# Row spread of the SSD mixer in four row groups and four banks, weight slots on 512-byte multiples, and another order of steps

## What is computed

```python
for l in range(DEPTH):                                   # DEPTH = 2
    h = rms_norm(x, attn_norm_w[l])
    proj = h @ w_in[l]                                   # 1024 x 2444
    a_q, a_k, a_v, b_z, b_xbc, b_dt, c_q, c_k, c_v = jnp.split(proj, offsets, axis=-1)
    y_a = windowed_gqa_sink(...)                         # 6 heads of 64
    y_b = ssd_mixer(b_z, b_xbc, b_dt, ...)               # 6 heads of 64, forward and backward
    y_c = diff_attention(...)                            # 4 heads of two maps of 32
    x = x + jnp.concatenate([y_a, y_b, y_c], axis=-1) @ w_out[l]
    h = rms_norm(x, ffn_norm_w[l])
    x = x + hierarchical_moe(h, ...)                     # 32 experts, 6 MB of weights each

# in ssd_mixer, for each of 6 heads and 2 directions:
da = jnp.cumsum(dt * a)                                  # over the tokens
seg = da[:, :, :, None, :] - da[:, :, None, :, :]        # every pair of tokens
decay = jnp.exp(jnp.where(lower, seg, -jnp.inf))
y_diag = jnp.einsum('bclsh,bcshp->bclhp', (C B^T) * decay, x * dt)
```

## Time and profile before

| what | value |
|---|---|
| median of three runs | 1198.58 us (1197.28 to 1199.71) |
| the profiled execution's own time | 1195.88 us, of which its span 1194.2 us |
| TensorE matmul busy | 933.3 us, 78% of the span |
| VectorE / ScalarE busy | 353.7 us (30%) / 203.0 us (17%) |
| bytes moved | 436.17 MB, mean 365 GB/s |
| mixer stage of layer 0 / of layer 1 | about 11 to 158 us / 600 to 747 us |

### The profile page before, as it was taken

The page is one execution under the profiler, slowest core; times in us unless marked ns, Lnnn a source line. Parts: engine busy times, 40 slices in busy tenths (PEclk is TensorE's granted clock), DMA queues, the critical chain, the costliest instruction groups (busy, mean ns, idle before and its releaser), DMA issues.

```text
span 1194.2 us, 26453 instructions
## 1 busy us (share of the span) xinstructions
PE 933.3 (78%) x11004; PEld 593.6 (50%) x11004; DVE 353.7 (30%) x1161; ACT 203.0 (17%) x600; POOL 8.0 (1%) x24
## 2 busy tenths in 40 slices
PE   7999989667668786796799998986667666665854
PEld 6887755334334443453388777443334333333532
DVE  4656352111112222132155654321111111111213
ACT  2366211000001010010024652110000000000001
POOL 2000000000000000000000000000000000000000
PEclk9998989888789998998899999898787888888988
DMA  9853389999999999999997235899999999999995
GB/s 328 313 234 142 109 337 426 426 426 426 426 425 423 426 426 425 401 423 428 409 374 312 82 131 232 349 424 426 427 426 426 427 426 426 428 423 427 425 425 215
DMA packets 50633, 436.17 MB, mean 365 GB/s; under 512 B 9408, under 2 KB 13760, under 8 KB 24640
## 3 DMA queue, kind: packets, MB, share of 16 engines
q1 hardware_dynamic: 50496, 434.26, 87.8%
HBM read 433.20 MB, written 1.05 MB: 364 GB/s over the span
## 4 chain that ended last, share of the span: by engine, by line
PE 48%; DMA 36%; issue 5%; DVE 5%; SPq 3%; DVEq 2%; ACT 1%; another core or an unknown queue 0%; ACTq 0%
DMA ring<-in_w_up 32%; PE ps L622 14%; PE ps L710 7%; PE ps L638 5%; PE ps L853 5%; DMA ring<-in_w_down 3%; PE ps L647 3%; PE ps L590 3%; PE ps L726 2%; SPq L461 1%; PE ps L610 1%; PE ps L715 1%; SPq L463 1%; DMA ring<-in_w_in 1%; PE ps L822 1%
## 5 line engine op out<-in xcount | busy, mean ns | idle before, releaser
L622 PE MATMUL ps<-ring,xg 128*32 128x256 f32 x4352 | 319.8, 457 | 174.5 <-DMA ring<-in_w_up 166.6
L622 PEld LDWEIGHTS ps<-ring,xg 128*32 128x32 f32 x4352 | 173.0, 131 | 304.5 <-issue 245.2
L1203 DVE SCALAR_TENSOR_TENSOR th<-th,ps 128x128 f32<-128x128 f32 x72 | 20.7, 288 | 592.3 <-ACT th L975 592.3
L638 PE MATMUL ps<-ring,actT 128*32 128x256 f32 x2304 | 139.5, 382 | 14.2 <-issue 12.9
L975 ACT ACTIVATE th<-ps 128x128 f32<-128x128 f32 x72 | 20.0, 278 | 514.9 <-PE ps L622 480.1
L638 PEld LDWEIGHTS ps<-ring,actT 128*32 128x32 f32 x2304 | 68.9, 109 | 75.6 <-DVE actT L1207 22.6
L590 PE MATMUL ps<-xh,Pb 128*32 128x256 f32 x1152 | 80.7, 397 | 24.5 <-issue 21.3
L710 PE MATMUL ps<-hT,ring 128*128 128x256 f32 x416 | 93.3, 381 | 1.3 <-ACT hT L1012 0.8
L710 PEld LDWEIGHTS ps<-hT,ring 128*128 128x128 f32 x416 | 78.0, 190 | 14.6 <-issue 4.0
L647 PE MATMUL ps<-ysb,PwT 32*128 32x256 f32 x992 | 71.5, 402 | 0.0
L590 PEld LDWEIGHTS ps<-xh,Pb 128*32 128x32 f32 x1152 | 39.4, 113 | 49.1 <-issue 26.0
(11 more groups left out here) (259 smaller groups left out, 690.0 us busy)
## 6 DMA issues: line engine op xcount, KB each, us to landing
ring<-in_w_down SPq DMA_DIRECT2D x62, 2048.0 KB, 41.0
ring<-in_w_gate SPq DMA_DIRECT2D x60, 2048.0 KB, 45.0
ring<-in_w_up SPq DMA_DIRECT2D x60, 2048.0 KB, 46.5
ring<-in_w_in SPq DMA_DIRECT2D x6, 2048.0 KB, 16.5
ring<-in_w_out SPq DMA_DIRECT2D x4, 2048.0 KB, 19.6
ring<-in_w_gate SPq DMA_DIRECT2D x8, 1024.0 KB, 30.0
ring<-in_w_up SPq DMA_DIRECT2D x8, 1024.0 KB, 31.7
ring<-in_w_in SPq DMA_DIRECT2D x6, 1024.0 KB, 16.4
```

Of the source, the lines that this page charges most:

```text
L622: last = mm(b_gate[j * SLOTS:(j + 1) * SLOTS, 0:2 * GQ], tokens[:, k, :], ring[:, low:high + 1:high - low, o:o + GQ], start=(k == 0), stop ...
L638: last = mm(b_y[j * SLOTS:(j + 1) * SLOTS, 0:DQ], actT[:, c * SLOTS:(c + 1) * SLOTS], ring[:, slot, o:o + DQ], start=(c == 0), stop=(c == ...
```

## The change

- `ROWS` becomes `3 * 32 + 2 * S_H` = 108. The last loop of `dta` writes the 12 values four times instead of twice, at columns 0, 32, 64 and 96, so that `cumT` holds its sums on four groups of partitions.
- `rows.k` takes each of its four rows (two heads, two directions) from a group of its own and writes each to a bank of its own, columns 0 to 255. `tenants` gives it four banks. `seg.h.d` reads bank `("seg", h, d)`.
- The start of `ring` is rounded up to a multiple of 512 bytes. Before, it was a multiple of 64; by the sizes of what lies below it, it began 192 bytes past a multiple of 512.
- `ORDER` is another permutation of the same steps. Up to `par` and from `outA.3` on it is the same.

```diff
-ROWS = 32 + 2 * S_H
+ROWS = 3 * 32 + 2 * S_H
...
 ORDER = """
-    sq xT.0 xT.1 xT.2 xT.3 rs par xbc.3 xbc.0 conv.3 xbc.2 xbc.1 conv.0 silu.0 xbc.4 conv.2 conv.1 dc.0 conv.4 silu.1
-    aq.0 silu.2 silu.3 dc.1 dt silu.4 dta aq.2 ak cB cum cumT xs.0 aS.0 sc.0 sc.1 cb.0 seg.0.0 nm.0 nm.1 seg.0.1 seg.1.0
-    rows.0 row.0.0 z.0 row.0.1 aq.1 zs.0 pT.0 xs.1 v seg.1.1 sc.2 row.1.1 aS.1 row.1.0 sc.3 ck.0 y.0 cb.1 rows.1 seg.2.0
-    seg.2.1 z.2 lam yq.0 pT.1 seg.3.0 row.2.0 nm.2 row.2.1 seg.3.1 row.3.1 row.3.0 z.1 zs.2 zs.1 sc.4 seg.4.0 seg.5.0
-    nm.3 pT.2 row.4.0 seg.4.1 yq.1 aS.2 seg.5.1 rows.2 ck.1 sc.5 y.1 row.5.0 row.4.1 row.5.1 oa.0 cq.1 cq.0 nm.4 y.2
-    pT.3 yq.2 nm.5 cS.0 oa.1 sc.6 pT.4 pT.5 sc.7 sS nm.6 oa.2 yn sc.8 cS.1 sc.9 pT.6 sc.10 nm.7 sc.11 outA.0 pT.7 sc.12
-    nm.8 outA.1 od.0 pT.8 sc.13 outA.2 nm.9 pT.9 od.1 oS.0 oS.1 outA.3 cn outB.0 outB.1 outB.2 outB.3 xc2.0 xc2.1 xc2.2
-    sa.0 sa.1 xc2.3 sa.2 fT.0 sd fT.1 fT.2 fT.3 rs2 lg seed wt cnt xn2 rank ov route
+    sq xT.0 xT.1 xT.2 xT.3 rs par xbc.0 xbc.3 conv.0 xbc.2 silu.0 conv.3 xbc.1 aq.0 dc.1 conv.2 conv.1 lam xbc.4 silu.1
+    silu.2 conv.4 dc.0 dt silu.3 dta silu.4 ak aq.2 cum cB sc.0 aS.0 sc.1 cumT nm.0 cb.0 z.0 zs.0 seg.0.0 seg.0.1
+    row.0.1 v rows.0 aq.1 row.0.0 seg.1.0 seg.1.1 xs.0 pT.0 row.1.0 xs.1 row.1.1 sc.2 sc.3 seg.2.0 nm.1 aS.1 ck.0 nm.2
+    y.0 cb.1 rows.1 row.2.0 nm.3 yq.0 z.2 seg.3.0 seg.2.1 row.2.1 aS.2 seg.3.1 row.3.0 row.3.1 pT.1 sc.4 seg.4.0 zs.2
+    nm.4 z.1 seg.4.1 seg.5.0 zs.1 rows.2 y.1 seg.5.1 yq.1 ck.1 row.4.0 row.4.1 row.5.1 cq.0 row.5.0 pT.2 oa.0 sc.5 cq.1
+    y.2 pT.3 cS.0 nm.5 yq.2 pT.4 oa.1 sc.6 sc.7 sS cS.1 pT.5 nm.6 yn oa.2 pT.6 sc.8 sc.9 nm.7 sc.10 outA.0 pT.7 outA.1
+    sc.11 nm.8 sc.12 pT.8 sc.13 nm.9 od.0 outA.2 pT.9 oS.0 od.1 oS.1 outA.3 cn outB.0 outB.1 outB.2 outB.3 xc2.0 xc2.1
+    xc2.2 sa.0 sa.1 xc2.3 sa.2 fT.0 sd fT.1 fT.2 fT.3 rs2 lg seed wt cnt xn2 rank ov route
 """
...
     if step[0] == "rows":
-        return [("seg", 2 * step[1] + 1, d) for d in range(2)]
+        return [("seg", 2 * step[1] + a, d) for a in range(2) for d in range(2)]
...
+        base[0] = -(-base[0] // 512) * 512
         ring = sb("ring", [P, RING + LATE, CHUNK])
...
                         for a in range(2):
                             for d in range(2):
-                                r = slice(32 * d, 32 * d + 2 * S_H)
-                                c = 32 * d + d * S_H + 2 * s[1] + a
-                                last = mm(ps[BANK["seg", 2 * s[1] + 1, d]][:, a * SEQ:(a + 1) * SEQ],
+                                o = 32 * (2 * a + d)
+                                r = slice(o, o + 2 * S_H)
+                                c = o + d * S_H + 2 * s[1] + a
+                                last = mm(ps[BANK["seg", 2 * s[1] + a, d]][:, 0:SEQ],
                                           ident[r, c:c + 1].broadcast_to([2 * S_H, P]), cumT[r, d, :], start=True, stop=True)
...
-                        e, seg_rows, c = E[h % 2][d], ps[BANK["seg", h | 1, d]], d * S_H + h
-                        for t in range(TT):
-                            o = h % 2 * SEQ + t * P
-                            A(e[:, 2 * t, :], seg_rows[:, o:o + P], ACT.Relu, bias=cum[:, t, 0, c:c + 1], scale=-1.0)
-                        o = h % 2 * SEQ + (1 - d) * P
+                        e, seg_rows, c = E[h % 2][d], ps[BANK["seg", h, d]], d * S_H + h
+                        for t in range(TT):
+                            A(e[:, 2 * t, :], seg_rows[:, t * P:(t + 1) * P], ACT.Relu, bias=cum[:, t, 0, c:c + 1], scale=-1.0)
+                        o = (1 - d) * P
                         A(e[:, 1, :], seg_rows[:, o:o + P], ACT.Exp, bias=cum[:, d, 2, c:c + 1])
...
-                        for o in (0, ROWS - n):
+                        for o in range(0, ROWS, 32):
                             last = v.tensor_tensor(dta[:, :, o:o + n], dts[:, :, :],
                                                    aneg[:, :].unsqueeze(1).broadcast_to([P, TT, n]), ALU.mult)
```

## The result

The changed kernel takes 1185.64 us (median of four runs, 1185.0 to 1186.87) against 1199.14 us of the kernel before (1197.28 to 1200.2 over four runs). The ratio is 0.9894, 95% interval 0.9877 to 0.991: 13 us less, about two and a half times the 5.2 us that were forecast. The profiled execution took 1185.0 us with a span of 1183.3; before it was 1195.88 and 1194.2, so the two traces differ by 10.9 us, while the medians differ by 13.5. The trace of before is of a short execution of its kernel (1195.88 us, under the lowest of the four runs), the one after of an ordinary one; the 2 to 3 us between are in neither trace.

A forecast was written before the change was run, and what follows sets the result against it. Mixer stages bound by TensorE, expert stages by DMA. Spread 2.7, gap before `y.2` 0.4, tail 1.6, others 0, plus 0.5 for the clock: 5.2 us off, 1193.4 against the median; forecast 1191 to 1196, 8 in 10 from 1184 to 1199.

The forecast's parts named there:

- The bound: Whole kernel: time cut from a mixer stage comes off the total one for one; expert stages take what their bytes take.
- The spread: `rows.k` in four row groups: half the streaming, 0.46 us saved a step, 2.7 us over 3 steps and 2 layers.
- What feeds it: `cumT` and `dta` ahead of `rows.k`: two more writes, about +0.2 us on VectorE; cost 0, up to 0.3 a layer.
- The order up to `y.2`: New step order in the mixer stage: no new gap, `y.2` starts 1.55 us earlier a layer, 3.1 in all.
- The tail: `y.2` to `outA.0`: 13.0 us in both layers, saving 1.6 us in layer 0 and none in layer 1.
- The alignment: Ring start rounded to 512 bytes, expert stages' transfers: taken as 0, with bounds of nothing and 10 us.
- the sum: All savings together: 2.7 + 0.4 + 1.6 + 0 + 0 = 4.7, plus 0.5 for the clock chance, 5.2 us.
- Rival A: Expert stages: the aligned ring brings transfers to 431 GB/s, 15 us saved in all, 1183; chance 0.12.
- B: Mixer stages: savings eaten by a failed narrow wait or a low clock in the tail, 1196 to 1201; chance 0.17.
- C: ScalarE's queue behind `oa.0`: gaps and low clock before `outA.0`, deciding from about 2 us extra a layer, 1205; chance 0.06.
- D: `rows.k`: twelve rows in four groups run no more side by side than in two, 1196; chance 0.05.

The follow-up runs named there:

- e2_no_align: The changed kernel without the rounding, so the ring starts where it did before; 1192.96 us, ratio 0.9953 to the kernel before.
- e5_two_groups: The changed kernel with its order and four banks, but two row groups and the ring where it was before; ratio 0.9974 to the kernel before.
- e6_rows_only: The changed kernel with the old `ORDER` and the old place of the ring, keeping four row groups and banks; ratio 1.0006 to the kernel before.
- e13_after_again: The changed kernel itself, unaltered, run once more beside the filled kernels; ratio 0.9893 to the kernel before.
- e1_align_only: The kernel before with only the start of the ring rounded up to 512 bytes; 1192.72 us, ratio 0.995.
- e4_ring_64: The kernel before with the ring starting 64 bytes past a multiple of 512; its time isn't in the text, its 16 KB packets take 614.3 to 614.7 ns.
- e12_before_fill: The kernel before with three matmuls of 256 columns that nobody reads, issued ahead of `oa.2`'s wait; ratio 0.9987.
- e11_fill: The changed kernel with unread matmuls ahead of `yn`, `pT.6`, `od.1` and `oS.1`; ratio 0.9924 to the kernel before.
- e14_fill_late: The changed kernel with unread matmuls ahead of `od.1` and `oS.1` only; 1184.3 us, ratio 0.9872 to the kernel before.

## Why the prediction was right in the mixer stages and wrong in the alignment

1193.4 us was forecast and 1185.64 measured. That is on the right side and inside the wide range of 1184 to 1199, but outside the forecast's own 1191 to 1196, and a move of 12.9 us from the median of 1198.58 it started from (13.5 from that of all four runs), where 5.2 was forecast.

*The bound.* It held. The mixer stages' 5.0 us came off without being given back: with the unaligned ring (`e2_no_align`) the expert stage of layer 0 kept its 444.8 us.

*The spread.* Forecast 0.46 us a step, from `cS.0`'s sixteen records in four groups; measured 0.43, and eight records take the 0.71 us foreseen. `e5_two_groups` puts a price on it in the new order, 1.28 us a layer.

*What feeds it.* It costs nothing, as said: two more writes, four in 0.47 us, where two took 0.28. `dta` ends at 46.47 (46.6 forecast).

```profile
46.00 0.47 DVE L1340 TENSOR_TENSOR dta<-dts,aneg 128x24 f32<-128x24 f32 x4
```

*The order up to `y.2`.* Forecast 1.55 us a layer and no new gap; measured 1.6 in layer 1 and 1.9 in layer 0 (1.4 on the mean of its traces), and no gap. That the room is needed is shown by `e6_rows_only`: in the old order banks are waited for, 2.5 us, more than the 1.3 that the shorter spread saves.

*The tail.* The mechanism was right, the sizes only roughly. ScalarE's `oa.0` does stand waiting for the projection, 3.0 us of the 3 to 4 forecast:

```profile
92.79 0.77 ACT L1093 ACTIVATE hT<-ps 64x256 f32<-64x256 f32 x2 [3.03 <-PE ps L711]
```

Forecast gaps were 0.35, 0.45 and 0.85; measured 0.40, 0.36 and 1.06, and 0.20 before `oa.2`. Their sum, 2.02 us, is no smaller than the 2.0 of layer 0 before. The mis-sized term was the clock: I took 13.0 us for both layers, as if it fell for 3.4 us, and it didn't fall (12.23 and 12.22). That gave 0.8 us more in each layer. In layer 1 it was given back, and more: 1.7 us in `outA.3`, behind two gaps (0.44 and 0.75) that I had set down as unchanged in sum and therefore free. With the same two gaps `outA.3` of layer 1 kept the full clock in `e13_after_again` and layer 0 lost it, so part of this is chance. The stages as a whole came out at 5.0 us against 4.7 to 5.2, and that is luck in part: these two errors cancel.

*The alignment, the step that failed.* "I take 0, since the same placement reaches both rates: what lowers 431 to 426 isn't the placement." Alone it brings 0.5% (`e1_align_only`), 6 us, as much as all the rest; the changed kernel without it has the ratio 0.9953, 5.6 us, and the sum had said 4.7 to 5.2. The comparison was the mistake, twice. The 431 GB/s came from 6 us of a mixer stage, and that is no rate to compare 350 us with: in the same 6 us the rings of `e4_ring_64` and `e12_before_fill`, both unaligned, reach 437 and 440, and the changed kernel's aligned one 421; and the kernel before reaches 431 from 200 to 206 us too, amid the experts. And those 6 us lacked the condition that brings the cost out: two or three transfers were open, and 91% of the 16 KB packets took at most 612 ns even unaligned. With the experts eight or more are open, and the same unaligned ring's packets take 613 and 620. Rival A had the right mechanism, with an upper end of 10 us where 6 were measured, and I gave it 0.12. The rule of the Trainium skill that stood beside it (in "DMA: Bandwidth & Descriptors", How a descriptor splits into AXI transactions) pointed the right way with twice the size, and I set it aside as one on reads.

*The rivals.* B's waits didn't come in the new order (and its terms add up to 1197 to 1200, not 1196 to 1201). C's condition was there (`oa.0` waiting), its 2 us of additional gap were not. D is refuted by the 0.71 us.

*Open.* Why 64 and 192 bytes cost the same, and why the cost grows with the number of open transfers, wasn't found; the number goes with it in every unaligned trace, but no run varied it alone. Nor why the clock falls in `outA.3` in one execution's layer 1 and in another's layer 0 of the same program. The old order up to `y.2` with the new tail wasn't tried.

## What to carry to other kernels

Let the buffers that large, densely queued transfers fill begin on a multiple of 256 bytes: it is one line, and here it was worth half of a change of three parts. To tell whether a resource is at its limit, compare long stretches with the same work queued on it: both of the rows compared here had the DMA full, but one was 6 us long, with two or three transfers open instead of eight or more. Work laid side by side in four row groups takes four banks, so price the new waits for banks together with the saving, and be careful with gaps removed before a clock fall, since the fall may just come at the next one.

## What the runs showed of the hardware

- A 16 KB packet into a ring on a 256-byte boundary takes 611.0 ns with the experts, one on 64, 128 or 192 past it 614.3 to 614.7; 429 against 426 GB/s. The unaligned packets lengthen with the number of transfers open at once: up to 612 ns are 79% with two open, 34% with five, 13 to 19% from eight on. Packets that ran while TensorE was busy weren't longer than those while it was idle.
- Twelve-row fp32 matmuls of 256 columns in four row groups: eight records in a slot of 0.64 us, against 1.07 in two groups.
- The granted clock fell to 1.2 GHz within a single gap of 1.66 us in nine of ten cases, behind two of 0.44 and 0.75 us in four of eight, and behind one of 0.47 (`e5_two_groups`) and one of 0.40 (`e11_fill`). One program shows the fall in different layers in different executions.
- Matmuls that nobody reads, put ahead of a wait for an operand, were followed by a step at full clock in all six places (`oa.2` of `e12_before_fill`, `oS.1` of `e11_fill` and `e14_fill_late`, in both layers each), where `outA.3` without them was low in four of eight layers and the old tail in nine of ten; put behind a wait for a bank they only delay (`e11_fill`).
